# Turning the attention probabilities' 32x32 blocks: from a round trip through DRAM to 16 transfers a head within SBUF

## What is computed

```python
# layer 0: h = rms_norm(x); q, k, v, g = split(h @ a_w_in)
sc = einsum('bqhd,bkhd->bhqk', q, k) * scale + bias       # chunked, relative bias
p  = softmax(sc)
o  = einsum('bhqk,bkhd->bqhd', p, v)
x  = x + (o * silu(g)) @ a_w_out
# layer 1: k, v from rms_norm(x, kv_norm) @ kv_w; q, g from rms_norm(x, b_norm) @ b_w_in
decay = cum_logf[:, :, q0:end, None] - cum_logf[:, :, None, :end]
sc = where(causal, einsum('bqhd,bkhd->bhqk', q, k) * scale + decay, NEG_INF)
p  = softmax(sc);  o = einsum('bhqk,bkhd->bqhd', p, v);  x = x + (o * silu(g)) @ b_w_out
```

## Time and profile before

| | |
|---|---|
| median of 3 runs | 2416.14 us |
| the profiled execution | 2415.02 us, span of its core 2413.3 us |
| granted TensorE clock | 0.999 of full speed |
| TensorE busy | 2382.5 us, 99% |
| VectorE, ScalarE, GpSimd busy | 1790.6, 1194.7, 485.5 us |
| the chain that ended last | TensorE 80%, VectorE 4% |
| DMA issues `pr_scratch<-sc`, `pT<-pr_scratch` | 64 and 256 |

### The profile page before, as it was taken

How to read it: one execution, slowest core, us unless ns; L and a number is a source line. 1 busy time by engine, 2 the same in 40 slices (tenths; PEclk the granted TensorE clock), 3 DMA queues, 4 the chain that set the end, 5 groups by cost and what they waited for, 6 DMA issues and landing times.

```text
span 2413.3 us, 40530 instructions
## 1 busy us (share of the span) xinstructions
PE 2382.5 (99%) x16396; PEld 2125.5 (88%) x16396; DVE 1790.6 (74%) x2693; ACT 1194.7 (50%) x1747; POOL 485.5 (20%) x721
## 2 busy tenths in 40 slices
PE   8999999899999999999999999999999999999998
PEld 7999999788888888888888888888888888888887
DVE  8998797896767676767666679767576767676766
ACT  6555433665444444444444456544444444444445
POOL 1222114432311021012101111321032103101311
PEclk9999999999999999999999999999999999999999
DMA  8666763387877687677778766877697768867874
GB/s 223 178 167 172 201 185 92 100 226 197 212 196 203 186 224 204 189 201 209 201 204 204 213 183 191 212 216 200 194 225 199 205 184 232 203 193 200 216 201 122
DMA packets 770633, 468.49 MB, mean 194 GB/s; under 512 B 33904, under 2 KB 726256, under 8 KB 770448
## 3 DMA queue, kind: packets, MB, share of 16 engines
q1 hardware_dynamic: 752880, 430.16, 65.6%
q0 software_dynamic: 17568, 35.75, 6.3%
HBM read 449.93 MB, written 15.89 MB: 193 GB/s over the span
## 4 chain that ended last, share of the span: by engine, by line
PE 80%; DVE 4%; issue 1%; ACT 1%; POOL 0%; DVEq 0%; ACTq 0%
PE bank L295 39%; PE bank L299 20%; PE bank L325 5%; PE bank L326 5%; PE bank L329 5%; PE bank L1944 1%; PE bank L1955 1%; DVE splitb L260 1%; PE bank L1943 1%; PE bank L1956 1%; PE bank L275 0%; PE bank L277 0%; PE bank L276 0%; ACT splitb L254 0%; DVE splita L260 0%
## 5 line engine op out<-in xcount | busy, mean ns | idle before, releaser
L295 PE MATMUL bank<-xx,splitb 128*128 128x512 f32 x3328 | 1152.9, 394 | 1.4 <-DVE mix L2228 0.8
L260 DVE TENSOR_TENSOR splitb<-rawb,splitb 128x1024 fp32r<-128x1024 f32 x672 | 834.4, 1253 | 370.3 <-ACT splitb L254 363.9
L254 ACT ACTIVATE splitb<-rawb 128x1024 fp32r<-128x1024 f32 x672 | 701.3, 1055 | 528.9 <-PE bank L299 376.3
L299 PE MATMUL bank<-xx,splitb 128*128 128x256 f32 x3328 | 919.9, 276 | 0.0
L295 PEld LDWEIGHTS bank<-xx,splitb 128*128 128x128 f32 x3328 | 625.0, 188 | 131.4 <-DVE mix L2228 1.1
L299 PEld LDWEIGHTS bank<-xx,splitb 128*128 128x128 f32 x3328 | 625.0, 188 | 2.6 <-DVE splitb L260 0.3
L295 PE MATMUL bank<-oo,splitb 128*128 128x512 f32 x1008 | 343.7, 390 | 1.3 <-DVE gT L2293 1.2
L275 PE MATMUL bank<-xhl,splita 128*128 128x258 f32 (+1 forms) x1040 | 295.3, 284 | 11.5 <-DVE splita L260 10.6
L277 PE MATMUL bank<-xhl,splita 128*128 128x258 f32 (+1 forms) x1040 | 292.8, 282 | 0.0
L276 PE MATMUL bank<-xhl,splita 128*128 128x258 f32 (+1 forms) x1040 | 292.4, 281 | 0.0
L299 PE MATMUL bank<-oo,splitb 128*128 128x256 f32 x1008 | 278.3, 276 | 0.0
(11 more groups left out here) (298 smaller groups left out, 2368.3 us busy)
## 6 DMA issues: line engine op xcount, KB each, us to landing
rawb<-in_a_w_in_dram SPq DMA_DIRECT2D x256, 512.0 KB, 5.2
rawa<-in_w_in_dram SPq DMA_DIRECT2D x130, 512.0 KB, 5.1
rawb<-in_kv_w_dram SPq DMA_DIRECT2D x128, 512.0 KB, 4.9
rawb<-in_b_w_in_dram SPq DMA_DIRECT2D x128, 512.0 KB, 5.4
rawb<-in_a_w_out_dram SPq DMA_DIRECT2D x64, 512.0 KB, 5.3
rawb<-in_b_w_out_dram SPq DMA_DIRECT2D x64, 512.0 KB, 5.3
rawb<-in_w_out_dram SPq DMA_DIRECT2D x32, 512.0 KB, 5.0
pr_scratch<-sc POOLq DMA_DIRECT2D x64, 192.0 KB, 2.3
```

The costliest lines, as they stand in the source:

```text
L254: nc.scalar.activation(self.parts(at, h)[0], self.raw_half(at, h), ACT.Copy).then_inc(hi_ready, 1)
L260: nc.vector.tensor_tensor(lo, self.raw_half(at, h), hi.bitcast(F32), ALU.subtract).then_inc(lo_ready, 1)
L295: nc.tensor.matmul(out, hi[:, w], both(k).rearrange("p a t -> p (a t)"), start=start and k == 0, stop=False)
L299: last = nc.tensor.matmul(out[:, 0:SEQ], lo[:, w], both(k)[:, 0], start=False, stop=stop and k == 7)
```

## The change

`store` and `fetch` become one step, `move`: 16 transfers per head, SBUF to SBUF, each of one 32-row by 96-column piece. `turn_blocks` writes into a buffer of its own, `blocks_T`, and before it does so for a head it waits until all 16 transfers of every earlier head have landed. `maxima` and two other places lose their wait for `pr_stored`. POOL adds the next head's mask (`finish`) ahead of all the transfers of this head, where it stood between `store` and `fetch`. `fz` is now laid over the value buffer `vtm`, so at the start of layer 1 ScalarE's copy into `vtm` also waits for the stored gates (`f_out`).

```diff
-    fz = sbuf(ph, "fz", [AH, 4, SEQ])
+    fz = vtm[0:AH].rearrange("p t (a s) -> p (t a) s", a=2)
+    blocks_T = sbuf(ph, "blocks_T", [P, W3])
...
-                def store(g, j):
+                def move(g, j):
                     n = head_no(layer, g, j)
                     pool.wait_ge(tr_ready, n + 1)
-                    if n > 1:
-                        pool.wait_ge(pt_in, 16 * NQ * (n - 1))
-                    pool.dma_start(pr_d[n % 2].rearrange("b r j e -> (b r) (j e)"), sc[:]).then_inc(pr_stored, 16)
-
-                def fetch(g, j):
-                    n = head_no(layer, g, j)
-
-                    pool.wait_ge(pr_stored, 16 * (n + 1))
                     wait(pool, o_sum, n - 1)
-                    for b in range(NQ):
-                        pool.dma_start(pT[n % 2][QB * b:QB * b + QB, :].rearrange("r (b e) -> r b e", b=NQ),
-                                       pr_d[n % 2, :, :, b].rearrange("b r e -> r b e")).then_inc(pt_in, 16)
+                    for keys in range(NQ):
+                        for rows in range(NQ):
+                            to = slice(NQ_W * rows, NQ_W * rows + NQ_W)
+                            of = slice(NQ_W * keys, NQ_W * keys + NQ_W)
+                            pool.dma_start(pT[n % 2][QB * keys:QB * keys + QB, to],
+                                           blocks_T[QB * rows:QB * rows + QB, of]).then_inc(pt_in, 16)
...
                         if j < GH - 1:
                             ask(g, j + 1)
-                        store(g, j)
                         if j < GH - 1:
                             finish(g, j + 1)
-                        fetch(g, j)
+                        move(g, j)
...
-                        pe.wait_ge(pt_in, 16 * NQ * (head_no(layer, g, j) + 1))
+                        pe.wait_ge(pt_in, 16 * NQ * NQ * (head_no(layer, g, j) + 1))
...
                         wait(act, o_sum, head_no(layer, g, b * VB))
+                        if begin and layer:
+                            act.wait_ge(f_out, 16)
...
                     def maxima(j):
                         dve.wait_ge(sc_sum, n + 1)
-                        wait(dve, pr_stored, 16 * n)
...
                     def turn_blocks(j):
                         dve.wait_ge(p_ready, head_no(layer, g, j) * 2 + 2)
-                        v_.transpose(sc[:].rearrange("p (b m c) -> p b m c", b=NQ, m=3),
+                        wait(dve, pt_in, 16 * NQ * NQ * head_no(layer, g, j))
+                        v_.transpose(blocks_T[:].rearrange("p (b m c) -> p b m c", b=NQ, m=3),
                                      pr[:].rearrange("p (m b c) -> p b m c", m=3, b=NQ)).then_inc(tr_ready, 1)
```

More of the change, by code:

```diff
@@ L1514, in _build @@
         sem("sc_sum"), sem("sc_taken"), sem("max_ready"), sem("exp_ready"), sem("p_ready"))
-    tr_ready, pr_stored, pt_in, v_taken, o_sum, gate_ready = (
-        sem("tr_ready"), sem("pr_stored"), sem("pt_in"), sem("v_taken"), sem("o_sum"), sem("gate_ready"))
+    tr_ready, pt_in, v_taken, o_sum, gate_ready = (
+        sem("tr_ready"), sem("pt_in"), sem("v_taken"), sem("o_sum"), sem("gate_ready"))
     inv_col, inv_turned = sem("inv_col"), sem("inv_turned")
@@ L1528, in _build @@
     nf_d = nc.dram_tensor("nf_scratch", [AH, SEQ], F32, kind="Internal").ap()
-    pr_d = nc.dram_tensor("pr_scratch", [2, 4, 32, 4, 96], F32, kind="Internal").ap()
     SCALE = float(P) ** -0.5
@@ L1579, in _build @@
     pT = [sbuf(ph, f"pT{b}", [P, W3]) for b in range(2)]
-    NQ, QB = 4, 32
+    NQ, QB, NQ_W = 4, 32, 3 * 32
     f_parts = sc[:, 0:SEQ]
@@ L2265, in second_norms @@
                 dve.wait_ge(f_part, 1)
-                dve.wait_ge(pr_stored, 16 * AH)
                 tt(f_parts, FP, inv, ALU.mult).then_inc(f_scaled, 1)
@@ L2410, in _ @@
                 dve.wait_ge(norm_root, 4 + q)
-                dve.wait_ge(pr_stored, 16 * 2 * AH)
                 v_.reciprocal(invc[:, q:q + 1], invc[:, q:q + 1]).then_inc(norm_inv, 1)
```

## The result

The changed kernel takes 2480.93 us (median of 4 runs, 2479.88 to 2482.76) where the kernel before takes 2415.69 (4 runs). The ratio is 1.0273, with a 95% interval of 1.0261 to 1.0286: 65 us slower. The forecast of 2449 us had the direction, and half of the size; 2480.93 lies 0.9 us above its range. One of e8's ten executions, further down, took 8529.12 us at the full clock, for a reason that is not known; its ratio leaves that one out.

The account below looks back on a forecast made before the run. TensorE alone was taken to bound the attention layers. Layer 1's 22.4 us, layer 0's 7.4, the gates' 0.6 and pauses' 3.5 sum to 33.9 on 2415.0: 2449 us, 1.4% slower, range 2425 to 2480.

Parts of the forecast that it names:

- The bound and the gain: Attention layers: bound by TensorE alone; removing store and fetches gains nothing, at most under 2 us.
- Issue time d: GpSimd's time to issue one new transfer: 0.50 us, bounds 0.43 to 0.55, so 8.0 us a head.
- Landing: The last new transfer of a head lands 2.1 us after its issue; other bound 4.6.
- The formulas for head 3: Transpose lateness at head 3: 48 d - 15.4 us in layer 1, 48 d - 19.8 in layer 0, less 3.0 of slack.
- landing as slow as the fetch: Rival, 12%: transfers land in 4.6 us instead of 2.1, adding 20 us plus 7 at heads 6 and 7: 2476.
- The prediction's own sign for it: TensorE waiting at heads 6 and 7 instead of the early heads would show landing as the cause; no size given.
- The rounds: Early heads: one loop of table load, mask and issues, 14.9 us in layer 1 and 13.5 in layer 0.
- Slack of VectorE: After the transpose of head 3: VectorE can be 3.0 us late before TensorE waits.
- Heads 6 and 7: End of each group: the move needs 9.6 us of 11.2 available, hidden with 1.6 us to spare.
- Pauses: GpSimd's pauses in issuing, now within the early heads' loop: 3.5 us, half of 7.6.
- The gates' buffer: ScalarE's copy into vtm at the start of layer 1: 3.5 us late once, costing TensorE 0.6 us.
- VectorE holds up the issues: Rival, 5%: VectorE's scalings of pr delay GpSimd's issues by up to 0.5 us each, 12 us in all: 2461.

Follow-up runs that it names:

- e8: Changed kernel with eight of the sixteen transfers a head, keys 64 to 127 left out (zeros stand there): 2416.38 us, ratio 1.0010.
- e9: Kernel before with 144 added 12 KB transfers in the projections, in series or alone, within SBUF, into or out of DRAM: 2413.05 us beside 2412.14.
- e6: Changed kernel with only the first half of each weight load fetched in the two attention layers: 2441.45 us, ratio 1.0114.
- e7: Changed kernel with the sixteen transfers a head issued from SyncE's queue between its weight loads: 2660.98 us, ratio 1.1015.
- e3: Changed kernel with two table buffers, each table asked for one head earlier, and one blocks_T: 2461.88 us, ratio 1.0191.
- e4: Changed kernel with two blocks_T buffers and two table buffers: 2420.96 us, ratio 1.0025.
- e12: Changed kernel with 8 of the 16 transfers for heads 6 and 7 of each group only: 2469.07 us, ratio 1.0229.
- e5: Changed kernel with the DRAM store and four fetches put back, gates in their own buffer, no f_out wait for ScalarE: 2418.41 us, ratio 1.0017.
- e10: Changed kernel with eight small useless TensorE products added in each group in the wait for k(3): 2472.16 us, ratio 1.0239.
- e1: Changed kernel with one store and four fetches a head through DRAM put back, out of blocks_T, the rest kept: 2419.74 us, ratio 1.0020.
- e2: Changed kernel with two blocks_T buffers, so a transpose waits only for the transfers of two heads before: 2447.30 us, ratio 1.0130.

## Why the prediction was wrong

Right in its mechanism, a loop through GpSimd that is longer than a head's time; wrong in one term, the landing; and blind to the second loop and to the clock.

- **The bound and the gain**: right. TensorE bound the layers, and nothing was won.
- **Issue time d**: 0.50 us, measured 0.500. The bounds of 0.43 to 0.55 were wider than needed.
- **Landing: the step that failed.** "I take 2.1 from the issue of the last one ... the read of DRAM seems to be the slow part." It is 4.6. The prediction had both neighbours in the earlier trace rows and reasoned by the kind of memory. e9 shows that the memory hardly matters, e6 and e7 that the weight stream does. The traces show how, when each transfer's landing is set beside the number of weight loads on their way at the end of its issue (median us from issue to landing, and how many):

| weight loads on their way | 0 | 1 | 2 | 3 | 4 |
|---|---|---|---|---|---|
| the new transfers, changed kernel | 1.6 (154) | 2.1 (84) | 4.6 (422) | 5.1 (266) | 5.1 (98) |
| the same in e6 | 1.6 (285) | 2.0 (159) | 2.7 (519) | 3.0 (58) | 3.1 (3) |
| the same in e7 | 1.8 (779) | 2.2 (127) | 3.1 (84) | 4.9 (34) | |
| the fetches, kernel before | 2.0 (26) | 3.1 (28) | 4.8 (158) | 4.9 (23) | 5.6 (21) |
| the stores of `sc`, kernel before | 2.3 (42) | 2.4 (22) | | | |

The stores that I leaned on were issued when at most one weight load was on its way, and the gates' store (1.7) when none was. A read of DRAM that met none landed in 2.0 to 2.4 us. So the trace of the kernel before already had the answer, and the kind of memory was a coincidence of when each was issued. What the DMA engines do with a small transfer behind weights is not in the records. The estimate from the Trainium skill ("DMA: Bandwidth & Descriptors", Anatomy of one DMA), 2.03 us for 12 KB and the receipt heaviest for HBM, fails here in the same way: it is near the 1.6 with no weights on their way and half of the 4.6. The Trainium skill also says (same page, Issuing engines are not separate DMA queues) that transfers interleave on the same 16 engines whoever starts them. e7's row of the table agrees: issued by SyncE they land late beside weights too.
- **The sum with 4.6 in it.** The prediction's arithmetic holds. The formulas for head 3 give 48 x 0.5 - 15.4 + 2.5 - 3.0 = 8.1 us a group in layer 1 and 3.7 in layer 0: 32.4 and, with 2.6 for the first group, 17.4. Measured were 33.3 and 19.2. The rival "landing as slow as the fetch" had the price of 2476 and a chance of 12%; it is the case that came true, with 5 us still missing. That it comes so near is in part luck: it counts the table's round in layer 0, where the landing's binds, and has no term for the clock. The prediction's own sign for it, TensorE waiting at heads 6 and 7, was there: 11.3 us at L1949.
- **The rounds.** One loop a layer was worked out. There are two: over the table (14.0 us measured, 14.9 forecast) and over the landing (0.9 + 7.85 + 4.6 = 13.3). With 2.1 for the landing the second is 10.8 and never binds, so the one error hid the other: e3, with this loop alone, is 47 us slower than the kernel before, and 41 slower than e4.
- **Slack of VectorE**: 3.0 us forecast. At head 3, lateness less what is left of it at head 5 is 2.6 us in three groups and 1.2 to 2.1 in the others, where TensorE kept more. Near, but 0.4 us or more too large in each group.
- **Heads 6 and 7**: "hidden with 1.6 us to spare" had the failed landing in it. With 4.6 the margin is negative by 0.9 us, 7 us in all, and a pause in issuing there is paid in full: 12.9 us with the gates' share, 11 back in e12. One of them, GpSimd in the first group of layer 0:

```profile
742.33 3.96 POOL L1836 DMA_DIRECT2D pT<-blocks_T  x8 [6.23 <-DVE blocks_T L2317]
748.62 3.92 POOL L1836 DMA_DIRECT2D pT<-blocks_T  x8 [2.33 <-issue]
```

- **Pauses**: 3.5 us forecast. The changed kernel has them (19.1 us of idling ahead of L1836 without a releaser: nine stops of 0.8 to 2.4 us and fourteen of 0.2). How much of it is hidden behind other work was not measured.
- **The gates' buffer**: 3.3 us late at the copy against 3.5 forecast; e5's time can't tell its price of 0.6 from nothing, but its place is right: the trace has 0.7 us of lateness behind the wait for the split at the end of q(0), as e5 shows by its absence.
- **The clock**: not in the prediction. It is about 9 us by e10, some of which sits inside the terms above, since the lateness counts it too.
- **VectorE holds up the issues**, a rival with 5% and 12 us: seen in kind, but tiny. The issues have 496 ns at the least, 498 in the median, 641 at the most. The four over 530 (546, 598, 603, 641) all lie beside VectorE's scalings of `pr`, and none of the 995 that touch no scaling is over 527; but only 29 touch one, and the sum is 0.4 us.

**Open.** e1, e4 and e5 still stand 4.5 to 6.4 us above the kernel before, at the full clock and with no wait of TensorE over 1.3 us in the attention layers. VectorE's wait in e1 and e5 and the gates in e1 and e4 are part of it. In e4 5.0 us appear as a TensorE that is busy for longer, 2387.5 us against 2382.5, in e1 3.2 us. Of these, 3.4 and 1.7 us lie in whole output projections. Leaving out e7 and the first group of layer 0, a group's takes 43.7 to 44.1 us, or else 45.4: two groups of e4, one of e1, e2 and the changed kernel, three of e3 and e10, one of e9. Nothing waits there and the granted clock is full; the products just follow one another more slowly. The same stretch of layer 0's second group before and in e4, 40 us of each:

```profile
985.00:1025.00 40.00, 40.00 (x238) 35.36 (x237) 28.41 (x32) 17.20 (x18) 0.00 (x0) 1.00 0.69 205
987.00:1027.00 40.00, 40.00 (x228) 34.69 (x227) 28.14 (x32) 16.11 (x16) 0.00 (x0) 1.00 0.68 201
```

228 products instead of 238. It strikes e9 as well, which is the kernel before with transfers added, so it may not belong to the change at all; what makes it was not found. In the changed kernel, too, the missing clock explains at most 15.4 of the 24.4 us of longer busy time.

## What to carry to other kernels

Price a small transfer's landing by a transfer that is issued with as many weight loads on their way, not by the kind of memory at its ends. When a serial step is made longer, list every closed loop that it stands in (here: the table's, and the landing of a buffer with one copy), because a second buffer for one only uncovers the next, and two together gave back 60 of 65 us. Waits of 2 to 3 us on a TensorE that is otherwise never idle can cost more than their length, so allow for time at the lower clock behind them.

## What the hardware showed

- A transfer of 12 KB within SBUF lands in 4.6 us beside the weight stream (1.6 to 6.2), in 2.3 beside half of it (1.6 to 3.8). With no weight load on its way it takes 1.6, with two 4.6. Beside the same number of loads, going into or out of DRAM made at most 0.4 us of difference in e9.
- GpSimd issues a transfer of 32 rows in 0.50 us, of 128 rows in 0.55. SyncE is no cheaper in e7: 0.59 us.
- GpSimd pauses for 1.2 to 2.1 us within its issues, with nothing that the profile shows: nine times in e4 over 1024 issues, 16.2 us in all.
- VectorE's scaling of `pr` can lengthen a transfer's issue by GpSimd, from 498 to at most 641 ns in the changed kernel.
- The changed kernel's layers have eight waits of TensorE of 2.3 to 3.4 us. At six of them the granted clock fell to 0.50 for some microseconds, at two it stayed at 1.00. In e12 it fell (0.66 over 5 us) at a wait of 1.95. Filling the idle time with products without use kept it at 1.00 in all places but one.
- TensorE can work through 40 us of products 4% more slowly, with no wait and a granted clock of 1.00 (228 products for 238 in e4).
